# One transformer layer with product-key experts: tokens innermost in the spread, 26 instead of 12 row pairs ahead of it, a quarter of the v rows on GpSimd

## The reference

```python
def peer_sublayer(h, w_pq, sub_keys1, sub_keys2, u_tab, v_tab, ln_g, ln_b):
    q = (xt @ w_pq).reshape(n_tok, PEER_HEADS, 2, PEER_HALF)
    s1 = jnp.einsum('thc,kc->thk', q[:, :, 0], sub_keys1)
    s2 = jnp.einsum('thc,kc->thk', q[:, :, 1], sub_keys2)
    v1, i1 = lax.top_k(s1, PEER_TOPK)          # 16 of 128 keys, twice
    v2, i2 = lax.top_k(s2, PEER_TOPK)
    ...                                        # the best 16 of the 16 x 16 sums
    experts = (e1 * PEER_KEYS + e2)            # 8 heads x 16 experts of 16384 for each token
    gate = jax.nn.softmax(sc, axis=-1)
    def chunk_fn(args):
        xc, ec, gc = args
        act = jax.nn.gelu(jnp.einsum('tkd,td->tk', u_tab[ec], xc), approximate=False)
        return jnp.einsum('tk,tkd->td', gc * act, v_tab[ec])
    ...
    return layer_norm(ALPHA * h + y, ln_g, ln_b)
```

## Time and profile before

| | us |
|---|---|
| median of 3 runs | 1991.41 |
| lowest to highest | 1988.37 to 1996.12 |
| the profiled execution | 1986.8 |
| its span | 1985.0 |
| PE (TensorE matmul) busy | 1764.8 (89%) |
| DVE busy | 1312.2 (66%) |
| POOL busy | 649.2 (33%) |
| ACT (ScalarE) busy | 202.5 (10%) |
| moved by DMA | 493.88 MB, 249 GB/s on average |

### The profile page before, as it was taken

One profiled execution on the slowest core, in us unless ns is written; L12 is line 12 of the kernel. 1 busy time (PEld: TensorE's weight loads), 2 busy tenths in 40 slices (PEclk: granted clock), 3 DMA queues, 4 the chain that ended last, 5 costly groups with the idle time before them and its releaser, 6 DMA issues.

```text
span 1985.0 us, 20568 instructions
## 1 busy us (share of the span) xinstructions
PE 1764.8 (89%) x7748; PEld 1324.3 (67%) x7748; DVE 1312.2 (66%) x2650; ACT 202.5 (10%) x422; POOL 649.2 (33%) x536
## 2 busy tenths in 40 slices
PE   7999999998999599999565899999999765799993
PEld 6587878887887488888465666666666565544441
DVE  3342273113265789953999877677877899976667
ACT  1101042000221021111000011011100000000000
POOL 1000000000034322212432574666476442475531
PEclk9999999999999799999655799999999755699996
DMA  6625102443389776767633699999999843599995
GB/s 210 223 64 149 64 1 82 144 162 122 112 286 346 289 251 230 251 233 276 202 117 96 225 409 409 409 409 409 395 407 409 318 118 95 184 410 409 409 409 210
DMA packets 193839, 493.88 MB, mean 249 GB/s; under 512 B 14103, under 2 KB 92952, under 8 KB 193444
## 3 DMA queue, kind: packets, MB, share of 16 engines
q0 software_dynamic: 74672, 271.55, 36.8%
q1 hardware_dynamic: 119068, 221.01, 31.2%
HBM read 489.32 MB, written 7.90 MB: 250 GB/s over the span
## 4 chain that ended last, share of the span: by engine, by line
PE 43%; DVE 22%; DMA 21%; issue 8%; POOL 5%; ACT 0%; SPq 0%; another core or an unknown queue 0%; DVEq 0%; ACTq 0%
PE ps L615 42%; DMA arena<-in_v_tab_dram,experts 17%; DVE arena L1308 7%; DVE arena L1286 3%; POOL arena L589 3%; POOL arena L580 3%; DVE arena L1275 2%; DMA arena<-in_u_cols_dram 1%; DVE hotg L1276 1%; DMA arena<-in_w_mem_kv_dram 1%; DVE arena L1274 1%; PE ps L627 1%; DVE arena L1276 1%; DMA arena<-in_w_in_dram 1%; DVE i L1209 1%
## 5 line engine op out<-in xcount | busy, mean ns | idle before, releaser
L615 PE MATMUL ps<-arena 128*128 128x256 f32 (+5 forms) x6272 | 1530.8, 406 | 66.4 <-DVE arena L1276 29.7
L615 PEld LDWEIGHTS ps<-arena 128*128 128x128 f32 (+2 forms) x6272 | 1116.8, 186 | 475.4 <-issue 259.8
L580 POOL DMA_INDIRECT arena<-in_u_tab_dram,experts x256 | 330.8, 1292 | 968.4 <-DVE dots L1286 568.6
L1308 DVE SCALAR_TENSOR_TENSOR arena<-arena,coef 128x1024 f32<-128x1024 f32 x254 | 327.0, 1287 | 102.0 <-DMA arena<-in_v_tab_dram,experts 97.8
L1286 DVE CUSTOM_DVE_ANT_0 arena<-arena 128x1024 f32<-128x1024 f32 x256 | 312.9, 1224 | 77.4 <-DMA arena<-in_u_tab_dram,experts 73.3
L589 POOL DMA_INDIRECT arena<-in_v_tab_dram,experts x256 | 307.1, 1200 | 151.5 <-DVE arena L1308 100.6
L615 PE MATMUL ps<-hotg,arena 128*128 128x64 bf16 x768 | 99.1, 301 | 93.1 <-DVE hotg L1276 93.1
L615 PEld LDWEIGHTS ps<-hotg,arena 128*128 128x128 bf16 x768 | 90.9, 146 | 101.0 <-DVE hotg L1276 101.0
L865 ACT ACTIVATE arena<-ps 128x256 f32<-128x256 f32 (+1 forms) x204 | 87.9, 438 | 677.5 <-PE ps L615 530.8
L1171 DVE TENSOR_TENSOR arena<-arena,ps 128x256 f32<-128x256 f32 x32 | 13.4, 420 | 125.9 <-PE ps L615 125.9
L1347 DVE TENSOR_TENSOR arena<-ps,arena 128x512 f32<-128x512 f32 x64 | 86.1, 1345 | 6.7 <-PE ps L615 6.0
(11 more groups left out here) (129 smaller groups left out, 812.6 us busy)
## 6 DMA issues: line engine op xcount, KB each, us to landing
arena<-in_u_cols_dram SPq DMA_DIRECT2D x128, 512.0 KB
arena<-in_v_tab_dram SPq DMA_DIRECT2D x128, 512.0 KB
arena<-in_w_in_dram SPq DMA_DIRECT2D x37, 1024.0 KB, 5.5
...
```

What stands on the lines that cost most here:

```text
L580: nc.gpsimd.indirect_dma_start(out=u_ring[:, n % ROWS, :], out_offset=None, in_=u_tab[0], in_offset=bass.IndirectOffsetOnAxis(ap=experts[: ...
L615: return nc.tensor.matmul(dst, lhsT, rhs, start=start, stop=stop, skip_group_check=True)
L1308: nc.vector.scalar_tensor_tensor(out=y_acc, in0=row, scalar=by, in1=y_acc, op0=ALU.mult, op1=ALU.add).then_inc(v_used, 1)
```

## The change

- `scatter` writes token t to every eighth column of the bank, from t on (`bank(key)[:, t:BT * CW:BT]`), so that the bank reads [unit, token]; `take_spread` reads it in a row and takes `acts` in its own order, runs of eight tokens at a step of 256 floats.
- `REST_PAIRS` goes from 12 to 26 (13 before ET and 13 after), `X_PAIRS` from 16 to 10 in each spread; V_PAIRS[0] stays 112, V_PAIRS[1] goes from 73 to 71.
- Every fourth v row (n % 4 == 3, 64 of 256) is no longer weighed by DVE. POOL scales it in place by its coefficient (`tensor_scalar`) and adds it to a second sum, `y_pool` (`tensor_tensor`); the first one of a tile is scaled straight into `y_pool`. It does so three pairs after it has issued the row's DMA, in the order of its own program, after waits for the coefficients, for the row, and for its own last operations. `gathered_norm` adds `y_pool` with one more DVE operation. Waits on `v_used` turn into waits on `v_used` or `v_pooled` by row.

```diff
@@ -61,12 +61,14 @@
 BT = 8
 BATCHES = GW // BT
 LAG = TOPK + 5
+TO_POOL = 4
+POOL_LAG = 3
 PAIRS_IN = GN * TOPK + LAG
 TOP_AT = 6
 TAIL_PAIRS = 32
 TOP_PAIRS = DN
-REST_PAIRS = 12
-X_PAIRS = (16, 16)
+REST_PAIRS = 26
+X_PAIRS = (10, 10)
 V_PAIRS = (112, PAIRS_IN - TAIL_PAIRS - TOP_PAIRS - REST_PAIRS - sum(X_PAIRS) - 112)
 FIRST_TOPS = 6
 TAIL_UNITS = 32
@@ -324,6 +326,7 @@
         vt_ring = at(156, 4 * TAB_RING).rearrange("p (j d) -> p j d", j=TAB_RING)
         acts = at(40, 64).rearrange("p (e t) -> p e t", e=CW)
         y_acc = hT[:, 4:8, 0:GW]
+        y_pool = hT[:, 0:4, 0:GW]
         onehots = arena[:, 8 * K:16 * K].bitcast(BF16)
         hot2 = onehots[:, 0:2 * BT * KEYS].rearrange("p (b e t) -> p b e t", b=2, t=BT)
         hot1 = onehots[:, 2 * BT * KEYS:2 * BT * KEYS + BT * CW].rearrange("p (e t) -> p e t", t=BT)
@@ -411,7 +414,8 @@
         dve_step = sem("dve_step")
         u_landed = [sem(f"u_landed{j}") for j in range(ROWS)]
         v_landed = [sem(f"v_landed{j}") for j in range(ROWS)]
-        u_used, v_used = sem("u_used"), sem("v_used")
+        u_used, v_used, v_pooled = sem("u_used"), sem("v_used"), sem("v_pooled")
+        coef_ready, row_scaled, y_read = sem("coef_ready"), sem("row_scaled"), sem("y_read")
         ut_landed = [sem(f"ut_landed{j}") for j in range(TAB_RING)]
         vt_landed = [sem(f"vt_landed{j}") for j in range(TAB_RING)]
         vt_used = sem("vt_used")
@@ -447,6 +451,19 @@
 
             g, i = divmod(s, DN)
             return scores[g][:, i, :]
+
+        def by_pool(n):
+            return n % TO_POOL == TO_POOL - 1
+
+        def pooled(n):
+            return n // TO_POOL
+
+        def wait_weighed(eng, n):
+
+            if by_pool(n):
+                eng.wait_ge(v_pooled, pooled(n) + 1)
+            else:
+                eng.wait_ge(v_used, n + 1 - pooled(n + 1))
 
         def landed_at(n):
             return 16 * (n // ROWS + 1)
@@ -585,19 +602,40 @@
             def v_row(s, k):
                 n = s * TOPK + k
                 if n >= ROWS:
-                    pool.wait_ge(v_used, n - ROWS + 1)
+                    wait_weighed(pool, n - ROWS)
                 nc.gpsimd.indirect_dma_start(
                     out=v_ring[:, n % ROWS, :], out_offset=None, in_=v_tab[0],
                     in_offset=bass.IndirectOffsetOnAxis(ap=experts[:, s, k:k + 1], axis=0)
                     ).then_inc(v_landed[n % ROWS], 16)
 
-            for p in range(PAIRS_IN):
+            def pool_weigh(n):
+
+                s, k = divmod(n, TOPK)
+                pool.wait_ge(coef_ready, s + 1)
+                pool.wait_ge(v_landed[n % ROWS], landed_at(n))
+                row = v_ring[:, n % ROWS, :].rearrange("p (a b) -> p a b", a=4)
+                by = coef[:, s % 2, k:k + 1]
+                if n % (HEADS * TOPK) == TO_POOL - 1:
+                    if n >= HEADS * TOPK:
+                        pool.wait_ge(y_read, 1)
+                    else:
+                        wait_full(pool, ("SC", 0, HEADS - 1))
+                    nc.gpsimd.tensor_scalar(y_pool, row, by, None, ALU.mult).then_inc(v_pooled, 1)
+                else:
+                    nc.gpsimd.tensor_scalar(row, row, by, None, ALU.mult).then_inc(row_scaled, 1)
+                    pool.wait_ge(v_pooled, pooled(n))
+                    pool.wait_ge(row_scaled, pooled(n) - n // (HEADS * TOPK))
+                    nc.gpsimd.tensor_tensor(y_pool, y_pool, row, ALU.add).then_inc(v_pooled, 1)
+
+            for p in range(PAIRS_IN + POOL_LAG):
                 if p < GN * TOPK:
                     if p % TOPK == 0:
                         pool.wait_ge(expert_ready, p // TOPK + 1)
                     u_row(*divmod(p, TOPK))
-                if p >= LAG:
+                if LAG <= p < PAIRS_IN:
                     v_row(*divmod(p - LAG, TOPK))
+                if p >= LAG + POOL_LAG and by_pool(p - LAG - POOL_LAG):
+                    pool_weigh(p - LAG - POOL_LAG)
 
 
         @block.tensor
@@ -823,7 +861,7 @@
                 begin(key)
                 for t in range(BT):
                     for i in range(3):
-                        last = mm(bank(key, t * CW, (t + 1) * CW), hot2[:, n % 2, :, t], hotg[n % 2][:, i, :, t],
+                        last = mm(bank(key)[:, t:BT * CW:BT], hot2[:, n % 2, :, t], hotg[n % 2][:, i, :, t],
                                   i == 0, i == 2)
                 last.then_inc(full, 1)
 
@@ -1291,30 +1329,39 @@
                 dve.wait_ge(gate_ready, s + 1)
                 c.link(nc.vector.reciprocal(gate_inv[:, s:s + 1], gate_sum[:, s:s + 1]))
                 dve.wait_ge(act_ready, s + 1)
-                c.link(nc.vector.scalar_tensor_tensor(
+                if s >= 2:
+                    dve.wait_ge(v_pooled, pooled((s - 1) * TOPK))
+                nc.vector.scalar_tensor_tensor(
                     out=coef[:, s % 2, :], in0=gate[:, s, :], scalar=gate_inv[:, s:s + 1],
-                    in1=act[:, s % 2, :], op0=ALU.mult, op1=ALU.mult))
+                    in1=act[:, s % 2, :], op0=ALU.mult, op1=ALU.mult).then_inc(coef_ready, 1)
+                dve.wait_ge(coef_ready, s + 1)
 
             def weigh(s, k):
 
                 n = s * TOPK + k
+                if by_pool(n):
+                    return
                 dve.wait_ge(v_landed[n % ROWS], landed_at(n))
                 row = v_ring[:, n % ROWS, :].rearrange("p (a b) -> p a b", a=4)
                 by = coef[:, s % 2, k:k + 1]
                 if n % (HEADS * TOPK) == 0:
                     nc.vector.tensor_scalar(y_acc, row, by, None, ALU.mult).then_inc(v_used, 1)
                 else:
-                    dve.wait_ge(v_used, n)
+                    dve.wait_ge(v_used, n - pooled(n))
                     nc.vector.scalar_tensor_tensor(out=y_acc, in0=row, scalar=by, in1=y_acc, op0=ALU.mult,
                                                    op1=ALU.add).then_inc(v_used, 1)
 
             def gathered_norm(i):
 
                 t = GATHER[i]
-                dve.wait_ge(v_used, (i + 1) * HEADS * TOPK)
+                n = (i + 1) * HEADS * TOPK
+                wait_weighed(dve, n - 2)
+                wait_weighed(dve, n - 1)
                 quarters = h[:, t, :].rearrange("p (a b) -> p a b", a=4)
                 c.link(nc.vector.scalar_tensor_tensor(out=quarters, in0=quarters, scalar=ALPHA, in1=y_acc,
                                                       op0=ALU.mult, op1=ALU.add))
+                nc.vector.tensor_tensor(quarters, quarters, y_pool, ALU.add).then_inc(y_read, 1)
+                dve.wait_ge(y_read, i + 1)
                 layer_norm(h_tile, [t], c, ln2_in, 32, out_ready)
 
             def pairs(lo, hi):
@@ -1343,8 +1390,8 @@
                 wait_full(dve, key)
                 if b == 0:
                     wait_done(dve, ("S", k * CW + CW - 1))
-                mine = acts[:, :, b * BT:(b + 1) * BT].rearrange("p e t -> p t e")
-                nc.vector.tensor_tensor(mine, bank(key).rearrange("p (t e) -> p t e", t=BT), mine, ALU.mult
+                mine = acts[:, :, b * BT:(b + 1) * BT]
+                nc.vector.tensor_tensor(mine, bank(key).rearrange("p (e t) -> p e t", t=BT), mine, ALU.mult
                                         ).then_inc(done, 1)
 
             dve_tail = [key for key, reader in tail_units() if reader == "dve"]
```

## The result

The changed kernel is slower: median 2055.47 us of 4 runs (2052.35 to 2058.88) against 1989.89 us of 4 (1987.86 to 1996.12), ratio 1.0325, 95% interval 1.0294 to 1.0355. The profiled execution took 2053.7 us, its span is 2051.9 us.

A forecast was written before the change was run, and what follows sets the result against it. The spreads were taken as bound by DVE, the table sums by transfers. Spreads −51, start +18.6, first sums +14, last stage −4, end +2.5 gave −19.9 us: 1971.5 us as a median, range 1938 to 2040.

The forecast's parts named there:

- my 3.2 us: Spreads: a batch without a row pair would take 3.2 us, set by TensorE's 3.11 us and the hand-over.
- C: Spreads: PSUM writes at a step of eight slow TensorE to 4.4 us a batch; 2024 us; chance 0.10.
- D: Spreads: TensorE gets 2.4 GHz, batches without a pair fall to DVE's 2.62 us; 1945 us; chance 0.10.
- B: POOL's work nearly free, under 3.7 us a pooled row, nothing lost in the sums; 1949 us; chance 0.13.
- W: POOL's time for one pooled row, scaling 1.03 plus add 2.06 plus steps and contention: 4.3 us, ends 2.7 and 7.2.
- E: Spreads: DVE's read is no faster in runs of eight tokens; +15 us, 1987 us; chance 0.05.
- The first one-hot: Ahead of the first spread: 14 more pairs, +2 us before ET and +16.6 behind; +18.6 us, ends +12 and +28.
- the ten rows that I had put at nothing: Five pooled rows in the spreads, five ahead of them: DVE's saving eaten by waits; nothing, between −13 and +18 us.
- A: Both table-sum stages: POOL becomes the bound at 5.5 us a pooled row, waiting for DVE; about 2033 us; chance 0.22.
- my own 46 us for each us of W: Table sums: each us of POOL time per pooled row costs 28 + 18 us, first stage and last stage.
- the −4 of the sum: Last stage: POOL's time with 18 pooled rows, 236 us, beside 241.2 − 5; −4 us, ends −5 and +49.
- The end: Last norm: one more operation, 1.3 us, and waiting for row 255 on POOL; +2.5 us together, between +1.3 and +5.

The follow-up runs named there:

- e1: Only the tokens-innermost layout, on the kernel before: 1966.3 us, ratio 0.989.
- e2: Only the row-pair counts (26 ahead of the first spread, 10 in each spread), on the kernel before: 1964.3 us, ratio 0.988.
- e4: Layout and row-pair counts together on the kernel before, without v rows on POOL: 1943.1 us, ratio 0.977.
- e9: New layout, no POOL rows, 14 pairs all before ET, 20 and 21 in the spreads, against the kernel before: 1929.6 us, ratio 0.970.
- e5: Kernel before with POOL operations appended behind the last store, no other engine working: scaling 2.85 us, add 2.34, copy 1.03.
- e7: Changed kernel with POOL writing four constant blocks per pooled row instead of scaling and adding; those v rows left out of the sum: 1963.7 us.
- e8: Changed kernel with POOL's waits kept but one written column per pooled row instead of scaling and adding; those rows left out: 1935.4 us.
- e10: Changed kernel with POOL writing five constant blocks per pooled row instead of scaling and adding; those rows left out: 1987.2 us.
- e11: Changed kernel with POOL writing six constant blocks per pooled row instead of scaling and adding; those rows left out: 2028.5 us.
- e12: Changed kernel with POOL making four copies that read the landed v row instead of scaling and adding; those rows left out: 2072.5 us.

## Why the prediction was wrong

**The layout and the counts: right, the spreads' total partly by luck.** Spreads of 121.0 and 129.2 us were forecast, 122.1 and 128.3 came; L1394 took 688 ns. e1 and e2 put the two parts at −23 and −25 us. But two errors met in the spreads. Batches with no pair ran faster than my 3.2 us, as TensorE's timeline shows in the first spread of the kernel after, with two windows of one batch each under it:

```profile
1070.17 3.10 PE L653 MATMUL ps<-hotg,arena 128*128 128x64 bf16 x24 [1.20 <-DVE hotg L1314]
1073.10 3.10 PE L653 MATMUL ps<-arena 128*128 128x64 bf16 x24
...
1081.26 3.12 PE L653 MATMUL ps<-arena 128*128 128x64 bf16 x24
1084.19 3.09 PE L653 MATMUL ps<-hotg,arena 128*128 128x64 bf16 x24
```

```profile
1070.20:1073.10 2.90, 2.90 (x25) 2.90 (x26) 2.41 (x4) 0.00 (x0) 0.00 (x0) 0.50 0.00 0
1084.20:1087.20 3.00, 3.00 (x26) 2.81 (x24) 2.75 (x5) 0.00 (x0) 0.68 (x1) 1.00 0.00 0
```

From 1070.17 to 1073.10 and from 1081.26 to 1084.19 it is 2.93 us from batch to batch: the recorded 3.11 us overlap. I had read the length of a batch as its pace; in the trace before, the first two batches begin 2.93 us apart too, at 966.80 and 969.73. Without POOL rows (e4) the spreads took 117.3 and 126.0 us; the pooled rows, which I had put at nothing in them, gave back 4.8 and 2.3 us of that.

**Rivals C and D fell together.** C wanted 4.4 us a batch from PSUM writes at a step of eight; the spread's matmuls take 302 to 303 ns on average stepped and 301 to 302 ns dense, and the batch comes every 2.93 us, as the two dense ones of before do. The Trainium skill, "PSUM — Partial Sum Buffer", Specifications, says that non-contiguous patterns slow matmuls significantly; these, 64 fp32 at a step of eight, weren't slowed. D's premise came true: the granted clock left 1.2 GHz (0.50) for 2.4 GHz in parts of the spreads, 0.73 and 0.74 on average. But a batch takes the same at either: 3.10 us recorded in the window at 0.50 and 3.09 us in the one at 1.00. My remark that weight loads seem to set the pace kept C's chance down, and should have done the same to D; that they do set it no run shows. B fell with W, which it wanted under 3.7 us, and E fell with the read's 688 ns.

**The first one-hot: +31.2 instead of +18.6.** Here the terms without POOL rows were short too: e4 has +25.5. There the transposes reach DVE at 942.36, 3.7 us later than before and not 2. TensorE does them later too (941.73 against 938.14), for its dots in front of them wait for table transfers; so the pairs in front of ET aren't shown to be the cause. In the changed kernel they reach DVE as early as before. Behind ET, DVE waits for rows. DVE's and TensorE's timeline in e4:

```profile
953.01 1.29 DVE L1308 SCALAR_TENSOR_TENSOR arena<-arena,coef 128x1024 f32<-128x1024 f32 x1 [1.08 <-DMA arena<-in_v_tab_dram,experts]
954.71 1.23 DVE L1286 CUSTOM_DVE_ANT_0 arena<-arena 128x1024 f32<-128x1024 f32 x1 [0.40 <-DMA arena<-in_u_tab_dram,experts]
```

```profile
992.31 3.12 PE L615 MATMUL ps<-arena 128*128 128x64 bf16 x24 [38.93 <-DVE arena L1276]
```

I priced a pair at the 2.38 us of five that ran freely. With more of them in a row DVE gets ahead of the transfers: gaps of 0.4 to 1.1 us, 3.7 us in all, and 2.56 us a pair behind them. TensorE idles 38.93 us there. e9 turns that round: no pair behind ET, and 14 us gained on e4 in the median although its spreads are 30 and 24 us longer. The other 5.7 us of the changed kernel's +31.2 come with the POOL rows; with the 4.9 and 2.4 us in the spreads that is 13 us for the ten rows that I had put at nothing, inside the bounds of −13 and +18.

**W, the step that failed.** I had said that the sign turns if POOL's two operations with their waits exceed 4.7 us. They took 5.75 us. Of the difference to my 4.3 us the scaling alone is the larger term: 2.85 us by itself (e5) where I took 1.03 from the cast. A cast and a multiplication by a coefficient have the same shape and one input; that they cost the same was an assumption that no row carried. For the add, double the cast was near (2.06 against 2.34). The value lay inside my ends of 2.7 and 7.2; what was wrong was the choice within them, and with it the chances of the forecast and of A. By my own 46 us for each us of W, 5.75 instead of 4.3 adds 67 us to the forecast of 1971.5: about 2038 us, slower than before, where 2055.5 came. So this one term turns the sign; the other 17 us are the sum of misses that partly cancel. In the first sums the corrected term gives +55 and +41.8 came, in the last stage +21 and +43.2 came, and the first one-hot came 12.6 us later than forecast. (For the last stage my figures, 236.4 beside 241.2, give −4.8 and not the −4 of the sum.)

**Rival A had the mechanism and, nearly, the W.** Its W was 5.5 us and its first sums +48 (measured +41.8). It named the wrong cause, for it blamed DVE rows held up in front of POOL; e5 shows that 5.19 us need no contention. And it gave 2033 us, 22 short of 2055.5, mostly in the last stage: +17 there, where +43.2 came. I had averaged POOL's slack over the whole of that stage. Its last part has only v rows, and there POOL has none to spare. POOL's timeline at its end:

```profile
1998.54 2.87 POOL L625 TENSOR_SCALAR arena<-arena,coef 128x1024 f32<-128x1024 f32 x1
2001.56 2.34 POOL L628 TENSOR_TENSOR arena<-arena 128x1024 f32<-128x1024 f32 x1
2004.05 1.81 POOL L606 DMA_INDIRECT arena<-in_v_tab_dram,experts  x1 [0.15 <-issue]
2006.16 1.02 POOL L606 DMA_INDIRECT arena<-in_v_tab_dram,experts  x1 [0.31 <-issue]
2007.49 0.94 POOL L606 DMA_INDIRECT arena<-in_v_tab_dram,experts  x1 [0.30 <-issue]
2008.74 0.94 POOL L606 DMA_INDIRECT arena<-in_v_tab_dram,experts  x1 [0.31 <-issue]
2009.71 2.87 POOL L625 TENSOR_SCALAR arena<-arena,coef 128x1024 f32<-128x1024 f32 x1
```

From scaling to scaling it is 11.17 us for four rows, each step following the last with at most 0.31 us between. From the last dot to the norm it took 1960.3 − 1915.2 = 45 us before and 2025.9 − 1957.9 = 68 us after: 23 of the stage's 43 us. Slack that POOL has while u and v rows alternate can't be carried there, since a ring holds five rows. e7 shows it without any reads: at 4.23 us a row it lost only 6 us against e8 in the first sums, but 22 in the last stage, 5.4 of them in the norm's wait for POOL (7.03 against 1.67 us).

**The cost I put at nothing.** That reads of POOL hold up DVE where transfers bound the stage I had put at nothing; only for ten rows in DVE-bound stretches had I left it a range. From the writes alone, W of 5.75 us lies between e10 and e11 at 1987.2 + 0.51 × 38.5 = 2007 us; the changed kernel takes 2055.5. Of the 120 us between e8 and after, about 71 would then be POOL's time and some 49 its reads beside DVE. That split is an estimate, interpolated between e10 and e11; that the second part exists e12 shows directly (44 us at equal POOL time).

**The end** came at +1.3 us behind the norm's start; the wait for row 255 is in the stage before it. In the profile the norm's first operation waits 8.37 us for POOL's last add, where I had put the whole end at +2.5. The norm of tile 0 I had left out: its wait of 10.03 us for POOL is shown with the result. The waits of this norm are 1.49 us in e8, 6.25 in e7, 9.79 in e10 and 9.60 in e11, and TensorE's stop behind it 0, 1.1, 10.9 and 18.4 us; that part of the loss isn't counted in POOL's busy time, in my sum or in a row's W.

**What stays open.** How the 49 us divide between DVE's longer rows and POOL's own issues (629 us in all after, 602 in e10 and in e11) wasn't taken apart. What the wait of tile 0's norm and TensorE's stop behind it cost wasn't taken apart either, so their share of the +41.8 us isn't known. Between e7, e10 and e11 the stop grows by 9.8 and 7.5 us while the first sums grow by 15.0 and 18.8. Nor does any run say why the slope is 15 to 18 us per microsecond of W in the first sums, with 27 pooled rows there, or why e10 lost nothing more than e7 in the last stage (260.1 against 257.4) and e11 then 25 us. Neither scaling the rows on ScalarE, which is busy a tenth of the span, nor a place further back for tile 0's norm was tried.
